# Mask, scale and negated maximum of three attentions in one VectorE pass over the score bank

## The reference, cut to what matters

```
# first block, 4 query blocks of 128, 8 heads
sc = einsum(q, k) * scale;  sc = where(mask, sc, -inf);  p = softmax(sc)      # mask: key chunk <= query chunk, chunks of 64
# second block, windowed ("a")
s = einsum(q, k) * D**-0.5; s = where(band, s, NEG)
m = max(s.max(-1), sink);   pr = exp(s - m);  denom = pr.sum(-1) + exp(sink - m)
# second block, sparse ("b")
_, sel = top_k(idx_score, 128);  s over the selected keys * D**-0.5;  p = softmax(s)
```

## Time and profile before

| | |
|---|---|
| time, median of 3 runs | 2005.54 us (2001.38 to 2006.76) |
| span of the profiled execution, first to last instruction | 2004.5 us |
| its own time | not listed apart from the three runs; the span lies 1.0 us under their median |
| instructions | 23848 |
| busy: PE, PEld, DVE, ACT, POOL | 1829.3, 1272.9, 936.2, 637.7, 175.7 us |
| mean granted TensorE clock | 0.966 of full speed |

### The profile page before, as it was taken

One profiled execution on the slowest core, in us unless ns is written; L12 is line 12 of the kernel. 1 busy time (PEld: TensorE's weight loads), 2 busy tenths in 40 slices (PEclk: granted clock), 3 DMA queues, 4 the chain that ended last, 5 costly groups with the idle time before them and its releaser, 6 DMA issues. The chain is left out here.

```text
span 2004.5 us, 23848 instructions
## 1 busy us (share of the span) xinstructions
PE 1829.3 (91%) x8828; PEld 1272.9 (64%) x8828; DVE 936.2 (47%) x1708; ACT 637.7 (32%) x1184; POOL 175.7 (9%) x261
## 2 busy tenths in 40 slices
PE   4997996898786899999999999979999999999996
PEld 2444676343334555767888878855667678888785
DVE  3687864332125786652222223358767332222334
ACT  2023551111112337621333322223574223332222
POOL 1000001111101450010000000024300000000001
PEclk8998997899998899999999999999999999999998
DMA  9262038799988000220333423240002213334231
GB/s 378 86 243 93 1 142 324 296 415 419 417 360 327 1 1 22 97 83 20 86 104 96 126 92 96 98 158 1 1 22 116 63 43 105 85 103 146 74 95 42
DMA packets 149213, 274.58 MB, mean 137 GB/s; under 512 B 10944, under 2 KB 108224, under 8 KB 135808
## 3 DMA queue, kind: packets, MB, share of 16 engines
q1 hardware_dynamic: 143648, 263.63, 36.4%
q0 software_dynamic: 5472, 9.70, 1.3%
HBM read 268.06 MB, written 15.20 MB: 141 GB/s over the span
## 5 line engine op out<-in xcount | busy, mean ns | idle before, releaser
L280 PE MATMUL bank<-ht_hi,gate_up_hi 128*128 128x512 f32 x704 | 274.1, 389 | 3.1 <-ACT arena L1518 3.1
L281 PE MATMUL bank<-ht_lo,gate_up_hi 128*128 128x512 f32 x704 | 273.9, 389 | 0.0
L282 PE MATMUL bank<-ht_hi,gate_up_lo 128*128 128x512 f32 x704 | 273.9, 389 | 0.0
L2590 PE MATMUL bank<-arena 128*128 128x512 f32 (+3 forms) x640 | 194.9, 463 | 6.4 <-ACT arena L1369 6.4
L2590 PEld LDWEIGHTS bank<-arena 128*128 128x128 f32 x640 | 113.7, 195 | 82.0 <-issue 64.1
L2198 DVE TENSOR_TENSOR arena<-arena,bank 128x512 f32 (+1 forms) x44 | 30.3, 688 | 272.2 <-ACT arena L1388 272.2
L280 PEld LDWEIGHTS bank<-ht_hi,gate_up_hi 128*128 128x128 f32 x704 | 132.1, 188 | 31.1 <-issue 3.9
L282 PEld LDWEIGHTS bank<-ht_hi,gate_up_lo 128*128 128x128 f32 x704 | 132.1, 188 | 27.7
L281 PEld LDWEIGHTS bank<-ht_lo,gate_up_hi 128*128 128x128 f32 x704 | 132.1, 188 | 27.3
L280 PE MATMUL bank<-down_hi,product_hi 128*128 128x512 f32 x352 | 138.1, 392 | 3.5 <-DVE arena L2198 3.5
L282 PE MATMUL bank<-down_hi,product_lo 128*128 128x512 f32 x352 | 138.1, 392 | 0.0
(11 more groups left out here) (384 smaller groups left out, 3076.7 us busy)
## 6 DMA issues: line engine op xcount, KB each, us to landing
gate_up_whole<-w_gu SPq DMA_DIRECT2D x88, 512.0 KB, 5.1
arena<-w_down_e SPq DMA_DIRECT2D x33, 1024.0 KB, 16.4
arena<-w_gate_e SPq DMA_DIRECT2D x32, 1024.0 KB, 18.4
arena<-w_up_e SPq DMA_DIRECT2D x32, 1024.0 KB, 20.5
down_whole<-w_down SPq DMA_DIRECT2D x44, 512.0 KB, 3.6
arena<-w_ada SPq DMA_DIRECT2D x5, 4096.0 KB, 21.3
arena<-w_in SPq DMA_DIRECT2D x4, 2048.0 KB, 17.6
w_o_whole<-w_o SPq DMA_DIRECT2D x2, 4096.0 KB, 13.8
```

The source lines that it names most:

```text
L280: pe.matmul(ps, xh, wh, start=start, stop=False)
L281: pe.matmul(ps, xh, wl, start=False, stop=False)
L282: return pe.matmul(ps, xl, wh, start=False, stop=stop)
L2590: ins = pe.matmul(ps[:, 0:b - a], HT[:, c, t * P:(t + 1) * P], w_in2[j][:, c], start=c == 0, stop=c == C8 - 1)
```

## The change

The mask products and the separate scale step go away. DVE makes one pass over each unit's bank that adds the mask (read from SBUF as bf16), multiplies by the negated scale, writes the result back in place and gives the minimum as the negated maximum: `out = (in0 + in1) * scale`, `accum = min(start, min(out))`. ACT's exponential then has the constant scale -1 in place of D**-0.5, or, in the first attention, in place of a scale read per partition. `y_neg` is signalled for each unit and not for each pair. The wait for the selection moves from PE to DVE. The masks become one tile of 256 columns (previous | own) and one of 512 (zeros, with the chunk mask at its end); the POOL memsets change accordingly.

```diff
@@ constants, POOL
-            own.mark(pool.memset(own_mask, 0.0))
-            own.mark(pool.memset(prev_mask, 0.0))
+            own.mark(pool.memset(window_mask, 0.0))
+            own.mark(pool.memset(first_mask, 0.0))
+            own.mark(pool.memset(first_mask[0:CHUNK, S - CHUNK:S], NEG))
@@ first attention, ACT
-                                         scale=hr[:, 0, t, h:h + 1], accum_out=lsum[:, t, h:h + 1])
+                                         scale=-1.0, accum_out=lsum[:, t, h:h + 1])
@@ second block, ACT
-                    y_neg.wait(act, l, i + 1)
                     for n in (2 * i, 2 * i + 1):
+                        y_neg.wait(act, l, n + 1)
-                                               scale=HD ** -0.5, accum_out=ls2[:, kk, t, h:h + 1]), ("s", kind, t, h))
+                                               scale=-1.0, accum_out=ls2[:, kk, t, h:h + 1]), ("s", kind, t, h))
@@ first attention, DVE row_max(n)
-                own.link(dve.tensor_reduce(mx[:, t, h:h + 1], ps[:, 0:(t + 1) * P], AX, ALU.max))
-                dve.tensor_scalar(nmx[:, t, h:h + 1], mx[:, t, h:h + 1], hss[:, 0, t, h:h + 1], None, ALU.mult).then_inc(s_negmax, 1)
+                dve.tensor_tensor_reduce(ps[:, 0:w], ps[:, 0:w], first_mask[:, S - w:], hss[:, 0, t, h:h + 1], LARGE, ALU.add, ALU.min,
+                                         nmx[:, t, h:h + 1]).then_inc(s_negmax, 1)
@@ second block, DVE row_max(n)
+                    if kind == "b" and t:
+                        if h == 0:
+                            y_sel.wait(dve, l, t)
+                        mask = SELM[:, t - 1, 0:w]
+                    else:
+                        mask = window_mask[:, 2 * P - w:]
-                    own.mark(dve.tensor_reduce(mx2[:, kk, t, h:h + 1], ps[:, 0:width(n)], AX, ALU.max))
-                    if h % 2 == 0:
-                        return
-                    own.settle()
-                    ... (L2118 or L2121 for the pair)
-                    y_neg.inc(ins)
+                    apart(dve)
+                    y_neg.inc(dve.tensor_tensor_reduce(ps[:, 0:w], ps[:, 0:w], mask, -(HD ** -0.5), nsinks[:, h:h + 1] if kind == "a" else LARGE,
+                                                       ALU.add, ALU.min, nmx2[:, kk, t, h:h + 1]))
@@ first attention, PE scores(n)
-                pe.matmul(ps[:, 0:w], QT[0:QK, h, t * P:w], KT[0:QK, h, 0:w], start=True, stop=False)
-                u1.full(pe.matmul(ps[:, t * P:w], ident_b, chunk_mask, start=False, stop=True), ("s", t, h))
+                u1.full(pe.matmul(ps[:, 0:w], QT[0:QK, h, t * P:w], KT[0:QK, h, 0:w], start=True, stop=True), ("s", t, h))
@@ second block, PE scores(pair)
-                        if kind == "b" and t and h == 0:
-                            y_sel.wait(pe, l, t)
-                        pe.matmul(ps[:, 0:w], turned["q" + kind, h // 2]..., keys..., start=True, stop=False)
-                    for n in pair:
-                        ... (L2657, or L2660 and L2661)
-                        u2.full(ins, ("s", kind, t, h))
+                        u2.full(pe.matmul(ps[:, 0:w], turned["q" + kind, h // 2]..., keys..., start=True, stop=True), ("s", kind, t, h))
```

More of the change, by code:

```diff
@@ L29 @@
 NEG = -1e30
+LARGE = 3e38
 HD = 64
@@ L339, in build @@
         chunk_mask = new(P, dt=BF16)
-        own_mask = new(P, dt=BF16)
-        prev_mask = new(P, dt=BF16)
+        window_mask = new(2 * P, dt=BF16)
+        prev_mask, own_mask = window_mask[:, 0:P], window_mask[:, P:]
         pos_i = new(2, T, dt=I32)
@@ L446, in build @@
         off += 256
+        first_mask = at(off, S, dt=BF16)
+        off += S // 2
         sig = at(off, 2, 512)
@@ L738, in build @@
         y_sel = Sig("selected", 3)
-        y_neg = Sig("negated_max2", 32)
+        y_neg = Sig("negated_max2", 64)
         y_pv = Sig("values_weighted2", 24)
@@ L1678, in row_max @@
                 t, h = divmod(n, NH)
+                w = (t + 1) * P
                 ps = u1.read(dve, ("s", t, h))
-                own.link(dve.tensor_reduce(mx[:, t, h:h + 1], ps[:, 0:(t + 1) * P], AX, ALU.max))
-                dve.tensor_scalar(nmx[:, t, h:h + 1], mx[:, t, h:h + 1], hss[:, 0, t, h:h + 1], None, ALU.mult).then_inc(s_negmax, 1)
+                dve.tensor_tensor_reduce(ps[:, 0:w], ps[:, 0:w], first_mask[:, S - w:], hss[:, 0, t, h:h + 1], LARGE, ALU.add, ALU.min,
+                                         nmx[:, t, h:h + 1]).then_inc(s_negmax, 1)
             def take_o(t):
@@ L2111, in row_max @@
                     kk = 0 if kind == "a" else 1
-                    ps = u2.read(dve, ("s", kind, t, h), l)
-                    own.mark(dve.tensor_reduce(mx2[:, kk, t, h:h + 1], ps[:, 0:width(n)], AX, ALU.max))
-                    if h % 2 == 0:
-                        return
-                    own.settle()
[L2117 to L2121, removed]
-                    y_neg.inc(ins)
+                    w = width(n)
+                    if kind == "b" and t:
[4 more added lines that the diff above has]
+                        mask = window_mask[:, 2 * P - w:]
+                    ps = u2.read(dve, ("s", kind, t, h), l)
+                    apart(dve)
+                    y_neg.inc(dve.tensor_tensor_reduce(ps[:, 0:w], ps[:, 0:w], mask, -(HD ** -0.5), nsinks[:, h:h + 1] if kind == "a" else LARGE,
+                                                       ALU.add, ALU.min, nmx2[:, kk, t, h:h + 1]))
                     if kind == "a" and h == 7:
-                        y_neg.wait(dve, l, n // 2 + 1)
+                        y_neg.wait(dve, l, n + 1)
                         y_sinkd.inc(dve.tensor_tensor(es2[:, t], nmx2[:, 0, t], sinks, ALU.add))
@@ L2649, in scores @@
                         ps = u2.begin(pe, ("s", kind, t, h), l)
-                        pe.matmul(ps[:, 0:w], turned["q" + kind, h // 2][p0:p0 + HD, t * P:(t + 1) * P], keys[p0:p0 + HD, k0:k0 + w],
-                                  start=True, stop=False)
-                    for n in pair:
[L2653 to L2661, removed]
-                        u2.full(ins, ("s", kind, t, h))
+                        u2.full(pe.matmul(ps[:, 0:w], turned["q" + kind, h // 2][p0:p0 + HD, t * P:(t + 1) * P], keys[p0:p0 + HD, k0:k0 + w],
+                                          start=True, stop=True), ("s", kind, t, h))
                 def turn_pair(p):
```

## The result

| | before | after |
|---|---|---|
| median of 6 runs each, us | 2005.95 (1999.59 to 2009.33) | 1991.36 (1985.65 to 1994.99) |
| span of the profiled execution, us | 2004.5 | 1989.2 |
| mean granted TensorE clock | 0.966 | 0.963 |

The ratio is 0.9933, with a 95% interval of 0.9914 to 0.9952: 13 us faster, with 10 to 17 in the interval. The forecast was 1991.

The account below looks back on a forecast made before the run. PE was taken to bound most steps and DVE some. The second block's 11.6 us plus the first attention's 3.0 made 14.6 off the 2004.5 us span, 1989.9, so a median of 1991; range 1985 to 2002.

Parts of the forecast that it names:

- PE's step: Second block: removing mask products brings PE's next start forward, 6.2 us a layer, 5.3 after steps held by other engines.
- The drain: Second block: full-height loads wait for half-height products; transposes inherit that wait. Rival that it hid the masks: 2001.5, chance 0.10.
- the early exponential: Second block: ACT's first exponential may start after one pass (0.5 us), not the pair (1.0); all latencies together 0.5 a layer.
- The new pass: DVE: costs the maximum of its width plus 0.06 us with a scalar. Rival heavier by a fixed amount: about 1996, chance 0.14.
- second cycle: DVE: rival that writing into the bank it reads takes two cycles a column, +1.07 ns each: 2013 us, chance 0.13.
- DVE's load hardly moves: Second block: a windowed pair costs DVE 0.87 us before and 0.88 after; sparse pairs 0.76.
- The 1.2 us then close: Second block: PE's 1.2 us a layer of waiting for ACT's exponentials before products of width 256 would close.
- The hold shifts rather than shrinks: Second block: PE's 2.19 us wait for DVE's `take_o` before the key transposes comes earlier but stays; counted as nothing.
- First attention: Its units shorten through PE, DVE and ACT savings: 3.0 us in all, bounds 2.0 and 4.5.
- Units of t = 0 and 1: First attention: a loop of two units through all three engines shortens by 0.3 us; 0.1 taken a unit.
- Units of t = 2: First attention: DVE sets the pace; 0.72 us before the taps becomes 0.62, so 0.10 a unit.
- Units of t = 3: First attention: bound by DVE, then PE; 0.06 to 0.10 us a unit, 0.07 taken.

Follow-up runs that it names:

- the experiment on the pair's wait: Kernel after, but ACT waits for the negated maxima of both heads of a pair before its first exponential: 1993.29 us, ratio 0.9947.
- the reordering in both kernels: In DVE's step 8 `take_o` put ahead of the pick: on the kernel after 1986.63 us, on the kernel before 2002.44 us.
- the column experiment: Kernel after, with the scale of the first attention's exponential read from a column of -1.0 instead of a constant: 1990.69 us, ratio 0.9929.

## Why the prediction was right, and where it wasn't

**PE's step.** Right in each width. Width 256 was to lose 0.18 us and lost 0.17 to 0.19; 384 0.28 and 0.28; 512 0.39 and 0.39; 128 0.07 and 0.07. The drain stayed and the transposes inherited it, and this is where the reading of start times in the earlier trace rows paid. Putting the masks back cost 4.7 us outside the hold's steps, against 5.3 forecast for all steps of a layer. Part of the 4.7 is the early exponential, which is worth less beside the masks.

**The new pass.** Forecast 0.42 to 0.48 us at 256 columns and 0.69 to 0.75 at 512; measured 0.42 to 0.47 without a scalar column and 0.49 with one, and 0.72 in the second block, 0.76 in the first. Writing into the bank that it reads cost no second cycle. The rule quoted from the Trainium skill (Vector Engine (DVE) Microarchitecture Reference, "Points that are easy to get wrong") speaks of two non-bf16 SBUF sources; at 1.04 ns a column nothing of a halving shows here, with one source in a bank and the other bf16. The convolution's taps, with two fp32 sources in SBUF and no accumulator, take 749 ns for 512 columns and show no halving either; a pass with both sources in SBUF and an accumulator was not run. One detail was off: the accumulator's read takes 142 ns, not the 82 of the earlier trace rows. It runs beside the next pass, so it costs nothing between passes. "DVE's load hardly moves" was off by a slip in the sum: the overlap of 0.08 us was taken off twice before and once after. In the list a windowed pair takes 0.81 us and not 0.88, where it took 0.87.

**The latencies.** "The 1.2 us then close" was wrong: PE still waits 1.2 us for exponentials before products of width 256. But pass and early exponential, put at 0.5 us a layer, gave 0.7 with the masks still on PE, since a wait elsewhere fell: step 14 went from 2.56 to 1.98 us with its masks still there, as PE's wait of 0.51 us for an exponential behind it closed. Taking the masks off gave that step nothing more: it is 1.98 us in the kernel after too, with a wait of 0.10. And the experiment on the pair's wait shows the early exponential to be worth 1.7 us once PE's step is short, 1.3 net of the hold. So this term was too small, and what is left for the masks without it (74.1 - 70.4 = 3.7 us outside) too large; the two help each other and can't be priced singly. Together they come to 5.5 in the undisturbed layer for 5.8 forecast. I forecast that ACT's idle time of 7.5 us would fall by half or more. It is 6.9: DVE's passes came earlier, and so did ACT.

**`take_o`.** "The hold shifts rather than shrinks: I count nothing for it" was the step that failed. Counted from the layer's first product, DVE releases PE 0.6 us earlier than before (22.68 and 23.31 us) but PE arrives 1.1 us earlier (20.02 and 21.12). So 0.47 us of the gain turned into waiting: the layer gave 5.5 of 6.0. With the reordering in both kernels it gives 5.7, and there the hold is still 0.35 us longer after than before (0.97 and 0.62), which makes 6.0 again. The forecast of 5.8 had no such term.

**The clock behind the hold.** The prediction had nothing on it. In the seven profiles whose hold was 2.2 us or more, the clock fell in 10 of 14 layers, from 2.0 us before the hold's end to 1.9 us behind it, which cost 0.8 to 1.8 us each where the same layer is at hand without a fall; in the four profiles with a hold of 1 us or less it never did. The Trainium skill (TensorE: Matmul & The Clock Gate, "Part 1: The HAM clock gate") says that an idle array is set back to half of its pulses and that the moment isn't tied to the kernel's own start; layers with one and the same hold that kept or lost the clock agree. Layer 2's 3.7 us is 5.5 less such a fall.

**First attention.** Forecast 3.0, measured 4.0 in the stage and 3.7 from first to last product. The mechanism was right, two terms were small. The other 0.2 to 0.3 us of the stage lie between the last score product and the first product behind the stage: 11.8 and 11.9 us in the two profiles with the old first attention, 11.3 to 11.7 in the seven with the new one in which the clock fell there. No term of the forecast covers that piece, and why it is shorter stays open. Units of t = 0 and 1: 22.21 to 20.27 us, 1.9 for 1.6. Units of t = 2: 17.9 to 16.6, 1.25 for 0.8, since the forecast took 0.62 us from pass to taps and the accumulator's overlap makes it 0.54. Units of t = 3: 0.54 for 0.56. The exponential's part is 0.8 us by the column experiment, forecast 0.7. The Trainium skill (ScalarE: Activation LUTs, "What ACT_TABLE_LOAD costs") gives some 93 ns for each operand of an activation that is read from a column; 564 less 474 ns agrees.

**The total.** 4.0 and twice 5.5 make 15.0 us where the clock holds; the forecast was 14.6. The medians differ by 14.6 us too, but that the two agree to the tenth is luck: the falls of the clock in and between the layers move single runs by more than the terms' errors.

## What to carry to other kernels

Price an instruction that is taken off a busy engine by the shift of the next start, width by width, and then look for the next wait with a release of its own: what PE gained here beyond DVE's gain turned into a longer hold. When a change brings one engine ahead of another, reorder the other's list in the same breath; here two swapped calls gave 1.7 us a layer beside the rewrite's 5.5, and took away an idle time that now and then cost the clock. Where whole runs scatter by 0.3%, a stage timed between its own events tells 0.1 us.

## What was not expected of the hardware

- With an idle time of PE of 2.2 to 3.9 us amid dense work the clock fell in 10 of 14 layers, during it or up to 1.9 us behind it, for some 3 to 7 us; with one of at most 1 us it never did, in eight layers.
- The fused pass with write-back into the bank runs at 1.04 ns a column, starts every 0.41 us at 256 columns with a scalar column, and its accumulator read of 142 ns is hidden.
- Behind products with 64 rows of weights the next load of 128 rows waits for "issue", 0.33 us in a step of width 256, whether a mask's load or a transpose's comes next: 6.5 and 4.0 us a layer over the masks' loads before, 8.1 over the transposes' loads after.
